# Two mixers in one program per engine, and the first rows scaled by VectorE before they are turned

## What is computed

```python
def first_block(x, ...):
    u = rmsnorm(x, norm_mix_g) @ w_in
    o_sb = sb_group(u[..., :SB_IN], sb_out_g)      # stick-breaking attention, 8 heads of 64
    o_rw = rwkv7_group(u[..., SB_IN:], ...)        # a recurrence with a 64x64 state per head, 8 heads
    h = x + concatenate([o_sb, o_rw], -1) @ w_out
    return rmsnorm(h + hier_moe(rmsnorm(h, norm_ffn_g), ...), final_norm_g)

def stick_breaking_attention(q, k, v):             # per block of 128 queries
    z = q @ k.T / sqrt(64)
    log_rest = where(s < t, log_sigmoid(-z), 0)
    suffix = cumsum(log_rest, reverse=True) - log_rest
    weights = where(s < t, exp(log_sigmoid(z) + suffix), 0)
    return weights @ v                             # then an rmsnorm per head, times sb_out_g

def rwkv7_scan(r, w, k, v, kk, a):                 # per token
    state = state * w + (state @ -kk) (kk * a)^T + v k^T
    out = state @ r
```

## Time and profile before

| | us |
|---|---|
| median of three runs | 1428.21 |
| lowest and highest | 1426.41, 1436.25 |
| the profiled execution | 1425.01 |
| its span in the profile | 1423.3 |

### The profile page before, as it was taken

One profiled execution on the slowest core, in us unless ns is written; L12 is line 12 of the kernel. 1 busy time (PEld: TensorE's weight loads), 2 busy tenths in 40 slices (PEclk: granted clock), 3 DMA queues, 4 the chain that ended last, 5 costly groups with the idle time before them and its releaser, 6 DMA issues. The chain is left out here.

```text
span 1423.3 us, 26018 instructions
## 1 busy us (share of the span) xinstructions
PE 1302.1 (91%) x11290; PEld 853.9 (60%) x11290; DVE 503.5 (35%) x938; ACT 361.5 (25%) x673; POOL 305.5 (21%) x349
## 2 busy tenths in 40 slices
PE   8999989888899999998979999998899899989893
PEld 7878764577745554444448887886545664444331
DVE  5267435432242421111184056662623500010006
ACT  2323136444133111111141232232533201111112
POOL 8345312255000200000014342450000110111000
PEclk9999999999999999999999999999999899999997
DMA  6811100300052799999971211102124569999994
GB/s 196 328 60 59 60 1 0 120 4 4 4 198 102 284 415 417 417 416 417 416 293 36 85 60 60 61 1 78 42 88 197 208 257 368 409 412 408 416 393 195
DMA packets 75448, 284.06 MB, mean 200 GB/s; under 512 B 15059, under 2 KB 16410, under 8 KB 63042
## 3 DMA queue, kind: packets, MB, share of 16 engines
q1 hardware_dynamic: 68752, 267.46, 48.2%
q0 software_dynamic: 5008, 10.64, 2.0%
q10 hardware_dynamic: 1570, 4.24, 0.8%
HBM read 258.49 MB, written 29.06 MB: 202 GB/s over the span
## 5 line engine op out<-in xcount | busy, mean ns | idle before, releaser
L390 POOL TENSOR_TENSOR arena_mix<-ring 128x512 f32<-128x512 f32 x52 | 70.0, 1364 | 174.2 <-PE banks L425 128.1
L1713 PE MATMUL banks<-ring,mixT 128*128 128x512 f32 x224 | 99.1, 595 | 3.9 <-PEq L50 3.1
L2069 POOL DMA_INDIRECT expert_rows<-arena_moe x21 | 20.5, 976 | 370.2 <-ACT arena_moe L2880 187.1
L435 ACT ACTIVATE arena_mix<-banks 128x256 f32<-128x256 f32 x104 | 39.4, 382 | 235.9 <-PE banks L425 235.9
L425 PE MATMUL banks<-ring 128*128 128x256 f32 x416 | 96.2, 380 | 1.6 <-DVE arena_mix L446 1.0
L446 DVE SCALAR_TENSOR_TENSOR arena_mix<-banks,arena_mix 128x256 f32<-128x256 f32 x78 | 31.9, 422 | 158.4 <-ACT arena_mix L435 89.0
L425 PEld LDWEIGHTS banks<-ring 128*128 128x128 f32 x416 | 78.3, 190 | 14.0 <-issue 3.6
L2086 PE MATMUL banks<-G_moe,x_hi_moe 128*128 128x256 f32 (+2 forms) x320 | 81.7, 295 | 1.2 <-DVE G_moe L2130 1.1
L2086 PE MATMUL banks<-G_moe,x_lo_moe 128*128 128x256 f32 (+2 forms) x320 | 80.0, 289 | 1.6 <-issue 1.6
L425 PE MATMUL banks<-ring,arena_mix 128*128 128x256 f32 x320 | 73.1, 383 | 0.7 <-ACT arena_mix L435 0.7
L2823 DVE TENSOR_TENSOR mixT<-mixT,banks 128x256 f32<-128x256 f32 x17 | 7.2, 421 | 187.7 <-ACT mixT L2862 187.7
(11 more groups left out here) (521 smaller groups left out, 2581.1 us busy)
## 6 DMA issues: line engine op xcount, KB each, us to landing
ring<-in_w_in SPq DMA_DIRECT2D x26, 1024.0 KB, 7.4
arena_moe<-in_exp_w_gate SPq DMA_DIRECT2D x16, 1024.0 KB, 14.8
arena_moe<-in_exp_w_up SPq DMA_DIRECT2D x16, 1024.0 KB, 17.3
arena_moe<-in_exp_w_down SPq DMA_DIRECT2D x16, 1024.0 KB, 16.3
ring<-in_exp_w_gate SPq DMA_DIRECT2D x16, 1024.0 KB, 13.4
ring<-in_exp_w_up SPq DMA_DIRECT2D x16, 1024.0 KB, 16.0
ring<-in_exp_w_down SPq DMA_DIRECT2D x16, 1024.0 KB, 13.8
arena_moe<-in_w_gate SPq DMA_DIRECT2D x8, 2048.0 KB
```

Of the source, the lines that this page charges most:

```text
L390: pool.tensor_tensor(out[:, c], a[:, c], b[:, c], op).then_inc(ph.sem("weight_sums"), 1)
L435: act.activation(self.dest(n, i)[block], self.m.banks[a][:, 0:256], ACT.Copy, scale=self.scale(n)).then_inc(ph.sem(name), 1)
L1713: last = pe.matmul(m.banks[k % 3][:], m.mixT[:, c, i * P:(i + 1) * P], w[:, c, :], start=(c == 0), stop=(c == DC - 1), skip_group_check=True)
L2069: pool.indirect_dma_start(z.d.outputs, bass.IndirectOffsetOnAxis(ap=place[:, c:c + 1].bitcast(U32), axis=0), z.y[:, 2 * c:2 * c + 2, :].re ...
```

## The change

Three things. In the first rows VectorE scales the whole row tile (128x1024) into `x.scaled`, which held only ScalarE's squares, and TensorE turns the scaled rows by transposes against the plain identity; the diagonal is gone. The two mixers share one block: each engine runs its suffix program and goes on with its recurrent one, with no meeting between. And the last steps of the suffix mixer are set among the first of the recurrent one:

- TensorE: after unit 11's suffixes and values(10): products(0), products(1), values(11), turn(0), products(2), squares(3), turn(1), turn(2), then products(i) and turn(i) for i from 3.
- VectorE: the ten constants before softplus(11); then mask(0), normed(2), masks 1 to 5, normed(3), masks 6 on.
- ScalarE: weights(11), inverse(2), output(3), copy of turn(0), inverse(3), copy of turn(1) on.
- GpSimd: its suffix program, then waits for values(11).
- SyncE: the four w_out loads come at the start of the joint block.

Where the buffers lie over each other there are waits on the suffix mixer's semaphores, and constants, state parts and gates are placed behind queries, keys and values (`at = max(...)`). The core of the diff:

```diff
-def norm_first_pe(pe, ph, m, rows, diagonal, t):
+def norm_first_pe(pe, ph, m, scaled, t):
-    pe.wait_ge(ph.sem("spread"), t + 1)
+    pe.wait_ge(ph.sem("scaled"), t + 1)
...
-            last = pe.matmul(m.banks[k % 6][:, j * P:(j + 1) * P], rows[:, t, c * P:(c + 1) * P], diagonal[:, t, :], start=True, stop=True)
+            last = pe.transpose(m.banks[k % 6][:, j * P:(j + 1) * P], scaled[:, t, c * P:(c + 1) * P], m.ident[:])
...
-        dve.tensor_scalar(diagonal[:, t, :], m.ident[:], m.small[:, 12 + t:13 + t], None, ALU.mult).then_inc(ph.sem("spread"), 1)
+        dve.tensor_scalar(scaled[:, t, :], rows[:, t, :], m.small[:, 12 + t:13 + t], None, ALU.mult).then_inc(ph.sem("scaled"), 1)
...
-            values(count - 1)
-            squares(HC - 1)
...
             for u in range(count):
                 if u + 2 < count:
                     magnitude(u + 2)
+                if u == count - 2:
+                    constants()
                 if u + 1 < count:
                     softplus(u + 1)
-                if u >= per and u % per == 2:
-                    normed(u // per - 1)
-            normed(HC - 1)
-            dve.wait_ge(ph.sem("normed"), HC)
+                if u >= per and u % per == 2 and u < count - 1:
+                    Stick.normed(dve, u // per - 1)
...
     xp, at = m.view(at, 3, NT, 64)
+    at = max(at, x.sb + 3 * HC * S)
     mask6, at = m.view(at, 6, 64)
...
-                if i >= 2:
+                if i < 2:
+                    pe.wait_ge(sb.sem("weights"), 2 * (stick.units - 2 + i))
+                else:
                     pe.wait_ge(ph.sem("masked"), i - 1)
...
                 if k >= 4:
                     pe.wait_ge(ph.sem("rows"), k - 3)
+                elif k < 2:
+                    pe.wait_ge(sb.sem("weights"), 2 * stick.units)
+                elif k == 2:
+                    pe.wait_ge(sb.sem("squared"), stick.heads)
+                else:
+                    pe.wait_ge(sb.sem("logs"), stick.heads)
...
-            for i in range(len(tiles)):
-                products(i)
+            stick.tensor(pe)
+            products(0)
+            products(1)
+            stick.values(pe, stick.units - 1)
+            turn(0)
+            products(2)
+            stick.squares(pe, stick.heads - 1)
+            turn(1)
+            for i in range(2, len(tiles)):
+                if i >= 3:
+                    products(i)
                 turn(i)
...
+            pe.wait_ge(sb.sem("normed"), stick.heads)
             front_products(pe, m, 0, (0, 1))
...
+            stick.vector(dve, constants)
+            v.wait()
             dve.sem_inc(ph.sem("constants"), 1)
+            dve.wait_ge(sb.sem("exponents"), stick.units)
             for i, (p, t) in enumerate(tiles):
                 dve.wait_ge(ph.sem("products"), i + 1)
+                if i == NT:
+                    dve.wait_ge(sb.sem("values"), stick.units)
+                if i == NT + 2:
+                    stick.normed(dve, stick.heads - 1)
+                if i == 2 * NT:
+                    dve.wait_ge(sb.sem("normed"), stick.heads)
                 dve.tensor_tensor(...).then_inc(ph.sem("masked"), 1)
+                if i == 0:
+                    stick.normed(dve, stick.heads - 2)
...
+            stick.scalar(act)
+            stick.output(act, stick.heads - 1)
             for k, (kind, p) in enumerate(turns):
+                if k == 1:
+                    stick.inverse(act, stick.heads - 1)
                 act.wait_ge(ph.sem("turned"), k + 1)
...
-            act.preload_act_table_set(EXP_LN)
...
+            stick.gpsimd(pool)
+            pool.wait_ge(sb.sem("values"), stick.units)
             pool.wait_ge(ph.sem("constants"), 1)
```

More of the change, by code:

```diff
@@ L846, with stick_programs @@
 STICK_UNITS = [(3, 2), (1,), (0,)]
[L849 to L852 removed]
+def stick_programs(m, x, ph):
     at = x.free1
@@ L878, in diagonals, with tensor @@
         return buf[:, :, 0:n * P].rearrange("p r (c n) -> p r c n", n=P)
-    with nc.Block() as block:
-        @block.tensor
-        def _(pe):
+    class Stick:
+        heads, units = HC, count
+        @staticmethod
+        def tensor(pe):
             def scores(u):
@@ L918, in suffixes @@
                 last.then_inc(ph.sem("exponents"), 1)
[L920 to L939, removed]
             scores(0)
@@ L947, in _, with values, squares, scalar @@
                 if u >= 1:
-                    values(u - 1)
+                    Stick.values(pe, u - 1)
                 if u >= per and u % per == 1:
-                    squares(u // per - 1)
-            values(count - 1)
-            squares(HC - 1)
-        @block.scalar
-        def _(act):
+                    Stick.squares(pe, u // per - 1)
+        @staticmethod
+        def values(pe, u):
+            p, cs = units[u]
+            pe.wait_ge(ph.sem("causal"), u + 1)
+            if p and u % per == 0:
+                pe.wait_ge(ph.sem("output"), p)
+                pe.wait_ge(ph.sem("squared"), p)
+            for c in cs:
+                k = column(cs, c)
+                for r in range(2):
+                    h = 2 * p + r
+                    last = pe.matmul(out[64 * r:64 * r + 64, c * P:], x.vb[:, c, 64 * h:64 * h + 64],
+                                     wt2[:, u % 2, r, k:k + S - c * P], start=(c == NT - 1), stop=(c == 0),
+                                     skip_group_check=True)
+            last.then_inc(ph.sem("values"), 1)
+        @staticmethod
+        def squares(pe, p):
+            pe.wait_ge(ph.sem("squared"), p + 1)
+            if p:
+                pe.wait_ge(ph.sem("logs"), p)
+            pe.matmul(sums[:], m.same64[:], sq[:], start=True, stop=True).then_inc(ph.sem("sums"), 1)
+        @staticmethod
+        def scalar(act):
             def log_part(u):
@@ L968, in weights @@
                     act.activation(wt2[:, u % 2, r, 0:width(u)], z(u)[:, r, 0:width(u)], ACT.Exp).then_inc(ph.sem("weights"), 1)
[L970 to L980, removed]
-                act.activation(inv[:], sums[:], ACT.Ln, scale=1.0 / 64, bias=eps[:, 0:1]).then_inc(ph.sem("logs"), 1)
-                act.wait_ge(ph.sem("logs"), p + 1)
-                act.activation(inv[:], inv[:], ACT.Exp, scale=-0.5).then_inc(ph.sem("inverse"), 1)
             act.preload_act_table_set(EXP_LN)
@@ L992, in _, with output, inverse, vector @@
                 if u >= per and u % per == 0:
-                    output(u // per - 1)
+                    Stick.output(act, u // per - 1)
                 if u >= per and u % per == 2:
-                    inverse(u // per - 1)
-            output(HC - 1)
-            inverse(HC - 1)
-        @block.vector
-        def _(dve):
+                    Stick.inverse(act, u // per - 1)
+        @staticmethod
+        def output(act, p):
+            act.wait_ge(ph.sem("values"), per * (p + 1))
+            act.activation(m.mixT[:, p, :], out[:], ACT.Copy).then_inc(ph.sem("output"), 1)
+            if p:
+                act.wait_ge(ph.sem("sums"), p)
+            act.activation(sq[:], out[:], ACT.Square).then_inc(ph.sem("squared"), 1)
+        @staticmethod
+        def inverse(act, p):
+            act.wait_ge(ph.sem("sums"), p + 1)
+            if p:
+                act.wait_ge(ph.sem("normed"), p)
+            act.activation(inv[:], sums[:], ACT.Ln, scale=1.0 / 64, bias=eps[:, 0:1]).then_inc(ph.sem("logs"), 1)
+            act.wait_ge(ph.sem("logs"), p + 1)
+            act.activation(inv[:], inv[:], ACT.Exp, scale=-0.5).then_inc(ph.sem("inverse"), 1)
+        @staticmethod
+        def vector(dve, constants):
             v = Chain(dve, ph.sem("dve"))
```

59 lines of the change are left out of this document (31 added, 28 removed).

## The result

| | before | changed |
|---|---|---|
| median of four runs each, us | 1427.31 | 1409.87 |
| lowest and highest | 1422.43, 1436.25 | 1406.21, 1412.94 |
| ratio, 95% interval | | 0.9874 (0.9841 to 0.9906) |
| profiled execution, its span | 1425.01, 1423.3 | 1412.94, 1410.9 |

The changed kernel is faster by 1.3%, more than forecast: 1420 was predicted, and 1409.87 lies 3 us under the lower end of the range. These four were probably a favourable draw. Each of the three sets stands beside its own runs of the kernel before: by the means the changed kernel is 18.6, 11.4 and 15.7 us faster (4, 10 and 6 runs), and weighted by the numbers of runs on both sides 13.7, uncertain by 2.4.

A forecast was written before the change was run, and what follows sets the result against it. TensorE's chain was taken to bound the kernel, busy 1302 of 1423.3 us. Seam 7.0 + front 1.0 = 8.0 us off the profiled 1425.0 gives 1417.0; with the median 3.2 above the profiled run, 1420, range 1413 to 1428.

The forecast's parts named there:

- The seam: Between suffix and recurrent mixers: interleaved steps remove TensorE's waits and the clock's fall, products(3) at 267.8, gain 7.0 us.
- The constants: VectorE's ten, 1.69 us, move into its 2.86 us idle time before softplus(11): free.
- The front: First rows, scaled by VectorE and turned by transposes: +1.0 us, between 1.75 and -0.2.
- The walk: VectorE's steps in the first rows, timed in order: first projection at 14.3 us instead of 15.21.
- the scaling: VectorE scaling a whole row tile in the first rows: taken as 1.15 us each.
- My lower bound: Row tile scaling on VectorE: 0.67 us for 1024 elements, from 1337 ns for 2048.
- the 1.75: First rows: gain in us if TensorE is at 2.4 GHz when the projection begins, which then ends at 29.2.
- My first rival: Seam works, but the front gives nothing or costs a little, transposes running at 1.2 GHz: 1421 us; chance 0.25.
- the last step: Sum carried to the kernel's end: 7.0 + 1.0 = 8.0 us off 1425.0 gives 1417.0, median 1420.
- The clock at the seam (second): Rival: the clock falls between the mixers all the same, 1424 us if half the work is at 1.2 GHz; chance 0.15.
- Stalls of issue (third): Rival: issue stalls in each of the recurrent mixer's 16 tiles, 1.1 us each, cost 17.6: 1438 us; chance 0.05.
- A wait fixed in time (fourth): Rival: a wait further on keeps the gain from reaching the end, 1428 us, no change; chance 0.05.

The follow-up runs named there:

- experiment 4: Changed kernel's joint block with the mixers' steps one behind the other, no overlap, against the kernel before: 1424.75 us, ratio 0.9962; profiled three times.
- the halves: Changed kernel with row tile 0 scaled in two pieces and three constants made three units earlier, against the kernel before: 1415.47 us, ratio 0.99.
- experiment 1: Both kernels unedited, again: changed 1416.29 us, ratio 0.9917 to the kernel before; the kernel before against itself 1427.27 us, ratio 0.9989.

## Why the prediction was right or wrong

**The seam: right, in size and mechanism.** 7.0 was the sum, 7.4 the measurement. TensorE's steps stood as predicted, without a gap over 20 us, and the masks took 0.96. The parts differ a little: products(0) comes 0.3 late, for a reason I had set at nothing, and products(0) to products(3) takes 7.27 instead of the 7.96 that I had added up from durations which overlap at their ends.

**The constants: not free.** I put 1.69 us into an idle time of 2.86. They took 3.4, and softplus(11) started 0.44 late:
```profile
250.59 0.27 DVE L1390 MEMSET arena_mix<- 128x256 f32 x1
...
251.02 1.28 POOL L1059 TENSOR_TENSOR arena_mix<-arena_mix 128x512 f32<-128x512 f32 x1
...
251.06 1.66 DVE L1393 TENSOR_TENSOR arena_mix<-masks 128x384 f32<-128x384 f32 x1
...
253.89 1.21 DVE L1017 SCALAR_TENSOR_TENSOR arena_mix<-banks,arena_mix 128x1024 f32<-128x1024 f32 x1
```
Where these constants stood before, GpSimd had nothing to do, and the same instruction (then line 1368) took 0.55 us. Moved beside an addition of GpSimd's it took 1.66, and it ends (252.72) about 0.4 after that addition does (252.30). The Trainium skill (SBUF — State Buffer, SBUF: two separate sides) says that a VectorE instruction with two SBUF inputs and a GpSimd one that reads SBUF share a port pair, which the one that starts first holds for its whole length; this trace agrees: a wait of 1.28 - 0.04 and then about the normal half microsecond. A duration taken from a place where the neighbour idles holds only there; the cover of 2.86 was nearly used up.

**The front: right in mechanism, 1.1 to 2.0 us too small.** The forecast was +1.0; 2.1 to 3.0 came, 3.0 between the first two profiles: the vectors' transpose stands between 27.91 and 28.03 in eight of the ten profiles that scale the rows and transpose them (28.29 in the third profile of experiment 4, 28.50 with the halves), and between 29.99 and 30.90 in the three with the old front. The walk took one profile's moment for the clock's rise, about 12 us, as fixed, which is worth up to 0.9. Two terms failed. First the scaling: 1.15 us each was too much, 1.09 and then 0.79, 0.75, 0.75. The projection began 1.25 earlier than my walk said; 0.82 of that lies in the three scalings before it, 0.24 in the small steps between (0.53 a tile and not 0.65), and 0.2 in the start of the first one, at 6.58 and not 6.79. My lower bound from the earlier trace rows, 0.67, was the near one: the instruction at line 698 has the same two sides in SBUF, and half of its 1337 ns plus a part of the fixed cost is 0.75. I leant on line 716 instead, whose 533 ns for 512 elements belong to another form. The Trainium skill (VectorE: DVE Perf Modes, The perf-mode tier table) has a float32 tensor_scalar between SBUF tiles run at twice the rate of one element a cycle. With the fixed part of its breakdown (the same page, Side-by-side: where the cycles go) that gives, as an estimate, 0.70 us for 1024, and the trace agrees, 0.75.

Second the clock: I took 0.75 off the 1.75 for the case that TensorE enters the projection at 1.2 GHz. In none of the ten profiles does it: the first 8 records of the projection take 1.89 to 1.97 us. In the repeated profile of the changed kernel, transposes alone have run from 7.73 on, and their records shorten from 417 to 272 ns before the first product of the projection. Records of line 302, ns min/median/max:
```profile
L302 PE MATMUL banks<-ident,arena_mix x12: 417/417/473, 7.7 to 10.1; 128*128 128x128 f32 x12
```
```profile
L302 PE MATMUL banks<-ident,arena_mix x8: 272/272/330, 11.8 to 12.6; 128*128 128x128 f32 x8
```
The rule of the Trainium skill that I had weighed (TensorE: Matmul & The Clock Gate, Part 4: PE-mode transpose), that transposes don't count as busy in the way matmuls do, would have given a loss of 0.2; here transposes raised the clock on their own, before the projection in eight of the ten profiles and at its start in the other two, and the measurement decides. 1.75 + 1.25 = 3.0 is the whole front as against the first profile of before. (The spacings that I named, 0.23 and 0.12 us, are 0.21 and 0.11 in the rows; the sums used 1.9 and 1.0 a tile, which hold.) My first rival, the front at nothing, is out.

**What the sum left out: the rest of the run.** 3.0 + 7.4 = 10.4 (10.0 with the mean front), and 13.7 (uncertain by 2.4) was measured; the first four runs said 17.4 by their medians, and it is probably chance in them that carried the result out of the range. Of the 3 or 4 us left I can say where they may lie, not what brings them. Times at the low level in some stretches, added up from the traces, in us:

| profile | 30 to 250 | 250 to 300 | 300 to 420 | 420 to 760 | 760 to 1110 | 1110 to 1400 |
|---|---|---|---|---|---|---|
| before | 6.8 | 6.8 | 0 | 17.1 | 0 | 27.3 |
| before, repeated | 13.7 | 6.8 | 13.7 | 13.7 | 0 | 20.5 |
| changed | 13.7 | 0 | 6.8 | 17.1 | 3.4 | 26.3 |
| changed, repeated | 10.2 | 0 | 3.4 | 13.7 | 3.4 | 17.4 |
| changed, third | 3.4 | 0 | 0 | 17.1 | 3.3 | 34.0 |
| w_out loads held back | 3.4 | 0 | 3.4 | 23.9 | 23.9 | 23.9 |

Of these six profiles only the column of the seam follows the kernel; elsewhere falls come and go between executions of one program, and the spread of the runs goes with them. Over all runs of these studies, a straight line with an offset for each kernel gives 0.8 us of span for each 0.001 of mean granted clock, with some 2.4 us of scatter left over. In the two later sets, where the clock of every run is on record, the changed kernel's mean clock is 0.0039 and 0.0075 above that of before (0.0051, weighted) and its gain 12.9 us. The seam's 6.8 us account for 0.0024 of these 0.0051 and are in the 10.4; the other 0.0027 are some 2.2 us by that line, which makes 12.6. Whether the changed kernel really holds the clock more often behind the seam, or its runs were lucky, is open. The kernel with the w_out loads held back has the same path as far as the seam, and its 11 runs show no more than the seam's part: a mean clock of 0.9718, 0.0026 above that of the runs of before beside them, and 11.2 us gained by the means.

**Which steps failed.** The term that was surely mis-sized is the front's: +1.0 in the sum, 2.1 to 3.0 measured. With 3.0 there and 7.4 for the seam the sum would have said 1418, still inside the range. The other is the last step: I carried 8.0 us to the end as if the level of the clock were a constant of the kernel, and gave 0.05 to more than that. The runs show instead that executions of one program differ by 12 or 13 us (1405.8 to 1418.2 in the six of the last set, 1410.0 to 1423.5 in the ten before), so that the median of four could end 3 us under the range while the median of 20 stands at its edge.

**The rivals.** The clock at the seam (second) stayed at 1.00 in all eight profiles with the overlap. Stalls of issue (third): none between 256 and 276 us, where TensorE is busy 20.00 of 20, and products(3) to products(15) take 17.53 us in all three profiles of the changed kernel, 17.54 before. A wait fixed in time (fourth) would bring the lead over the profile of before to nothing somewhere. At 300 us, at 1110 and at the end it is 7.9, 9.0 and 12.1 us in the first profile of the changed kernel, 9.2, 7.0 and 9.6 in the second, 12.2, 15.1 and 16.9 in the third. It wanders as falls of the clock come and go, and nothing took it back.

## What to carry to other kernels

Where two phases meet, count three things apart: the waits that interleaving fills (5.0 us here), what the clock costs behind the wait where it falls (2.3), and the meeting itself (some 0.5); the first is what pays, and filling the wait saved the second as well, in eight profiles of eight. A float32 matmul against a diagonal, used only to turn and scale, costs two records where a transpose costs one: scale elsewhere if that engine has 0.75 us a tile to spare. Read the moment at which the clock rises from more than one profile before it goes into a sum: here it was worth 0.9 us. And take a duration for moved work from a place with the same neighbours: 0.55 us alone was 1.66 beside GpSimd.

## What the runs showed that I had not expected

- After the same wait of 2.23 us at the same place of the same program, the clock fell in one profile of three. In all, 3.4 to 10.2 us at the low level appeared at the start of the scores in each of the fourteen profiles, of nearly the same code there, costing some 1.2 us for each 3.4.
- 76 executions of the kernel before (and 12 more in experiment 1) lay between 1420.8 and 1442.9 us, a spread of 1.5% on one core; the ratios of 12 runs are good to 0.3% only.
- Transposes alone lifted TensorE from 417 to 272 ns a record.
- The old front's mark followed the clock's rise (29.99 with 10.4 us, 30.84 with 12.3, 30.90 with 12.4). The new front's hardly does: it stays within 27.91 to 28.03 for rises from 10.3 to 12.1, since TensorE waits there for VectorE's scalings anyway, and is 0.4 later (28.29) with a rise behind 13 us.
- Cutting one 128x1024 scaling in two raised it from 1.09 to 1.64 us.
